# Four norms of a two-block kernel: tokens scaled before they are turned, with new head, tail and decay sums

## The reference, cut to what matters

```python
def rmsnorm(x, g):                      # first block: mixing norm and FFN norm
    y = x * lax.rsqrt(jnp.mean(x * x, axis=-1, keepdims=True) + EPS)
    return y * g
h = rmsnorm_2(x, norm_mix_w) * (1 + sc_m) + sh_m      # second block, from c @ w_ada
z, xbc, dt_raw, q, k, v = jnp.split(h @ w_in, IN_SPLITS_2, axis=-1)
...
a_cs = jnp.cumsum(A, axis=2)                          # decay sums of the SSD scan
seg = a_cs[:, :, :, None] - a_cs[:, :, None]
...
h = rmsnorm_2(x, norm_ffn_w) * (1 + sc_f) + sh_f
x = x + g_f * conv_ffn(h, w_up, ffn_conv_w, w_down)
return rmsnorm_2(x, final_norm_w)
```

## Time and profile before

| | |
|---|---|
| median of 3 runs | 799.52 us (799.29 to 799.68) |
| the profiled execution | 799.78 us |
| its span (first to last instruction) | 797.80 us |
| TensorE busy | 786.4 us, 99% |
| VectorE busy | 599.5 us, 75% |
| ScalarE busy | 489.8 us, 61% |
| granted TensorE clock | 0.998 of full |
| read from HBM | 159.16 MB, 201 GB/s |

### The profile page before, as it was taken

The page is one execution under the profiler, slowest core; times in us unless marked ns, Lnnn a source line. Parts: engine busy times, 40 slices in busy tenths (PEclk is TensorE's granted clock), DMA queues, the critical chain, the costliest instruction groups (busy, mean ns, idle before and its releaser), DMA issues. The chain is left out here.

```text
span 797.8 us, 14220 instructions
## 1 busy us (share of the span) xinstructions
PE 786.4 (99%) x5912; PEld 735.6 (92%) x5912; DVE 599.5 (75%) x803; ACT 489.8 (61%) x746; POOL 17.8 (2%) x38
## 2 busy tenths in 40 slices
PE   8999999999999999999999999999999999999996
PEld 7999979999999889999998888999789999999885
DVE  5576686667876868797878897987968787777463
ACT  6878888567743564444434357767758767665451
POOL 3000001000200000000000000001000000000000
PEclk9999999999999999999999999999999999999999
DMA  8873534456444558898987993634362856555611
GB/s 303 293 245 126 199 124 155 159 180 243 159 159 159 163 208 264 277 303 277 306 289 266 343 373 132 231 107 159 106 211 85 257 163 206 165 170 173 237 53 53
DMA packets 105679, 161.13 MB, mean 202 GB/s; under 512 B 4480, under 2 KB 51856, under 8 KB 105616
## 3 DMA queue, kind: packets, MB, share of 16 engines
q1 hardware_dynamic: 105472, 159.97, 60.4%
q10 hardware_dynamic: 144, 0.26, 0.1%
HBM read 159.16 MB, written 1.06 MB: 201 GB/s over the span
## 5 line engine op out<-in xcount | busy, mean ns | idle before, releaser
L1759 PE MATMUL ps<-p1H,wH 128*128 128x256 f32 x1256 | 358.2, 286 | 1.5 <-issue 0.8
L1111 DVE TENSOR_TENSOR wL<-raw,wH 128x2048 fp32r<-128x2048 f32 (+2 forms) x142 | 284.6, 2009 | 98.4 <-ACT wH L705 94.6
L1759 PE MATMUL ps<-p1H,wL 128*128 128x256 f32 x1256 | 354.8, 283 | 0.0
L1759 PE MATMUL ps<-p1L,wH 128*128 128x256 f32 x1256 | 353.3, 283 | 0.0
L705 ACT ACTIVATE wH<-raw 128x2048 fp32r<-128x2048 f32 (+1 forms) x114 | 212.0, 1864 | 132.2 <-PE ps L1759 77.0
L1759 PEld LDWEIGHTS ps<-p1H,wH 128*128 128x128 f32 x1256 | 240.8, 192 | 5.9 <-issue 3.9
L1759 PEld LDWEIGHTS ps<-p1H,wL 128*128 128x128 f32 x1256 | 240.8, 192 | 0.0
L1759 PEld LDWEIGHTS ps<-p1L,wH 128*128 128x128 f32 x1256 | 240.1, 192 | 0.1
L1762 PE MATMUL ps<-wH,zH 128*128 128x512 f32 x168 | 65.4, 389 | 0.0
L1762 PE MATMUL ps<-wH,zL 128*128 128x512 f32 x168 | 65.4, 389 | 0.0
L1762 PE MATMUL ps<-wL,zH 128*128 128x512 f32 x168 | 65.4, 389 | 0.0
(11 more groups left out here) (296 smaller groups left out, 978.9 us busy)
## 6 DMA issues: line engine op xcount, KB each, us to landing
raw<-in_w_in SPq DMA_DIRECT2D x37, 1024.0 KB, 5.2
raw<-in_w_ada SPq DMA_DIRECT2D x24, 1024.0 KB, 5.2
raw<-in_w_up SPq DMA_DIRECT2D x44, 512.0 KB, 4.9
raw<-in_w_ffn_gate SPq DMA_DIRECT2D x22, 512.0 KB, 4.2
raw<-in_w_ffn_up SPq DMA_DIRECT2D x22, 512.0 KB, 5.6
raw<-in_w_ffn_down SPq DMA_DIRECT2D x10, 1024.0 KB, 5.6
raw<-in_w_down SPq DMA_DIRECT2D x10, 1024.0 KB, 5.2
raw<-in_w_out SPq DMA_DIRECT2D x8, 1024.0 KB, 5.0
```

What stands on the lines that cost most here:

```text
L1111: return v.tensor_tensor(o, a, b, op)
L1759: last = mm(ps[:, t[1], 0:T], wt[:, slot, k, t[2]:t[2] + P], at_[:, k0 + k, :], start=st, stop=en)
```

## The change

- **Norms 0 to 3.** `TMP`, `rb`, `rbs`, `spread` and `late_turn` go. VectorE scales the tokens by `R1` ahead of the turning, in five pieces (`scale_tokens`): token block 0 in two halves, block 1 in 256, 256 and 512 columns. TensorE turns the scaled tokens `US`. ScalarE reads each turned block twice: to `p1H` and, unrounded, to one of three buffers `un_full`, both with the weight (and shift) applied; VectorE subtracts.
- **TensorE's order in a norm.** First token block 0, then block 1 in pairs of k. In norms 1 to 3 all 16 turns stand ahead of the panel; in norm 0 blocks k 4 to 7 are turned inside `q0`. In norm 1 and 3 the second gate sum, in norm 2 the row of the modulation, stand between token block 0 and 1.
- **Head.** Token block 0 comes in two halves on SP, block 1 on ScalarE's queue. SP waits for the first half only. `warm` runs 8 and 2 times instead of 4, 2 and 4.
- **Tail.** In `dd1` the second tile's first parts are closed one panel earlier; VectorE adds them (`all_but_last_part`) ahead of the last panel's first tile. The left half goes to a bank of its own as well. Three of four stores' products are VectorE's; the last one is one operation from `res`, without `HG`.
- **Decay sums.** Four matmuls of 16, 16, 16 and 8 columns.

```diff
+            act.dma_start(res[:, 1], IN["x"][0, P:2 * P, :]).then_inc(on.in_x[2], 16)
...
@@ scalar: norm @@
-                act.wait_ge(on.ut_psum, 4 * n + 1)
-                nc.scalar.activation(TMP[:, 0], un(0), ACT.Copy).then_inc(on.un0_copy, 1)
                 if n == 0:
                     first_hi(0, 0, 1)
+                    act.wait_ge(on.in_par, 16)
...
-                    act.wait_ge(on.tmp_done, 8 * n + k + 1)
-                    if n < 2:
-                        nc.scalar.activation(p1H[:, k], TMP[:, k], ACT.Copy).then_inc(on.uh_done, 1)
-                    else:
-                        nc.scalar.activation(p1H[:, k], TMP[:, k], ACT.Identity,
-                                             bias=shift(n, k)).then_inc(on.uh_done, 1)
-                    if k == 0:
-                        act.wait_ge(on.rb_psum, n + 1)
-                        nc.scalar.activation(rbs, rb, ACT.Copy).then_inc(on.rb_copy, 1)
+                    act.wait_ge(on.ut_psum, 4 * n + k // 2 + 1)
+                    bias = dict(bias=shift(n, k)) if n >= 2 else {}
+                    f = ACT.Identity if n >= 2 else ACT.Copy
+                    nc.scalar.activation(p1H[:, k], un(k), f, scale=gain(n, k), **bias).then_inc(on.uh_done, 1)
+                    if k > 2:
+                        act.wait_ge(on.u_ready, 8 * n + k - 2)
+                    nc.scalar.activation(un_full[k % 3], un(k), f, scale=gain(n, k), **bias).then_inc(on.un_done, 1)
@@ vector: norm @@
+            def scale_tokens(n, j, cs):
+                dve.wait_ge(on.rd_done, 2 * n + j + 1)
...
+                v.tensor_scalar(US[:, j, cs], (Y if n == 2 else res)[:, j, cs], R1[:, j:j + 1], None,
+                                ALU.mult).then_inc(on.us_done, 1)
...
+                scale_tokens(n, 0, half(0))
+                scale_tokens(n, 0, half(1))
                 turn_over(n, 1)
+                scale_tokens(n, 1, slice(0, T))
+                scale_tokens(n, 1, slice(T, W))
+                scale_tokens(n, 1, half(1))
...
                 for k in range(KD):
-                    stt(TMP[:, k], un(k) if k else TMP[:, 0], gain(n, k), rbs if k else rb, ALU.mult,
-                        ALU.mult).then_inc(on.tmp_done, 1)
-                    if k > 1:
-                        low(k - 1)
-                    if n == 0 and 0 < k < 4:
+                    if n == 0 and k < 4:
                         first_lo(0, k, 1, k == 3)
-                    elif n == 0 and k == 5:
-                        first_lo(1, 0, 2, False)
-                    elif n == 0 and k == 6:
-                        first_lo(1, 2, 2, True)
+                    elif n == 0 and k in (5, 6):
+                        first_lo(1, 2 * k - 10, 2, k == 6)
                     elif n == 3 and k in (5, 7) or n == 2 and k == 6:
                         later_lo(n, 0 if k == 5 else 2)
-                low(KD - 1)
+                    low(k)
@@ vector: tail @@
-                        step(tt(gt[:, T:W], o[:, T:W], g[:, T:W], ALU.mult))
-                        step(tt(right, gt[:, T:W], right, ALU.add))
-                        turn_over(n, 0)
...
+            def all_but_last_part(name, n):
+                whole, o = res[:, 1, half(1)], ps[:, GROUPS[name]["tiles"][1][1], :]
+                dve.wait_ge(*USED[PIDX[name, len(GROUPS[name]["parts"]) - 2]])
+                dve.wait_ge(*EV["dd0", 1])
+                step(tt(gt, o, GATE[n - 3][1], ALU.mult))
+                step(tt(whole, gt, whole, ALU.add))
...
-                    scaled(1, 1)
+                    stt(OUT[:, 1, half(1)], res[:, 1, half(1)], R1[:, 1:2], gout[:, half(1)], ALU.mult,
+                        ALU.mult).then_inc(on.out_dve, 1)
@@ tensor: norm @@
+                    if n == 0:
+                        warm(8)
                     if n in GATE_OF:
                         gate_sum(GATE_OF[n], 0)
+                    pe.wait_ge(on.us_done, 5 * n + 1)
+                    turn(range(4), (0,))
                     if n:
+                        pe.wait_ge(on.us_done, 5 * n + 2)
+                        pe.wait_ge(*EV[f"{RES[n]}1", 1])
+                        turn(range(4, 8), (0,))
+                    if n in GATE_OF:
+                        gate_sum(GATE_OF[n], 1)
                     if n == 2:
                         ada_row(1)
+                    for x in range(4 if n else 2):
+                        pe.wait_ge(on.us_done, 5 * n + min(3 + x, 5))
+                        turn((2 * x, 2 * x + 1), (1,)).then_inc(on.ut_psum, 1)
@@ tensor: decay sums @@
-                        for x, terms in enumerate((((M0, 0),), ((M1, 0),), ((SL, 0),), ((SL, 0), (OL, 1)),
-                                                   ((M0, 1),), ((M1, 1),))):
-                            for y, (mat, j) in enumerate(terms):
-                                last = mm(ps[:, 7, 64 + 8 * x:72 + 8 * x], mat[:], ADT[:, j, :], start=y == 0,
-                                          stop=y == len(terms) - 1)
+                        mm(bm[:, 0:5:4], M0[:], ADT[:], start=True, stop=True)
+                        mm(bm[:, 1:6:4], M1[:], ADT[:], start=True, stop=True)
+                        mm(bm[:, 2:4], SL[:], ADT[:, 0:1].broadcast_to([P, 2, 8]), start=True, stop=False)
+                        last = mm(bm[:, 3], OL[:], ADT[:, 1, :], start=False, stop=True)
```

126 lines of the change are left out of this document (46 added, 80 removed).

## The result

| | before | after |
|---|---|---|
| median | 799.65 us (799.29 to 800.17) | 805.20 us (803.18 to 805.78, 5 runs) |
| the profiled execution, its span | 799.78 us, 797.8 us | 803.18 us, 801.5 us |

The ratio is 1.0066 [1.0054, 1.0077]: slower, and outside the range I gave (797.6 to 802.9). The profiled execution is the fastest of the five; the other four took 805.0 to 805.8 us. So there are two things to explain: the 3.7 us between the two spans, and 2 us more that four of five runs have.

A forecast was written before the change was run, and what follows sets the result against it. TensorE, busy 99% of the span, was taken as the bound, with other engines counting only at head, norms and tail. Terms -0.9 - 0.6 + 0.4 + 0.7 + 1.7 + 0.5 = +1.8 gave 801.3 us, range 797.6 to 802.9.

The forecast's parts named there:

- The norm before u0: Fourth norm: ScalarE's chain and VectorE's half weight difference start the fifth block later, +1.7 us, the largest term.
- The norm before xs: Third norm: TensorE idles for the scaled tokens, then turns, row and copy delay the first matmul, +0.7 us.
- The norm before f0: Second norm: first matmul at 291.17 instead of 290.92, block 1 waits 0.45; +0.4 us in all.
- The decay sums: Four matmuls instead of seven, eight instructions remaining at 0.106 us each: -0.6 us.
- The two-pointer reading: ScalarE's PSUM read with weight and shift as pointers: taken at 0.45 us, bounds 0.36 and 0.50.
- Rival 1: The chains stay hidden and only TensorE's own list counts: -2.0 us, 797.5; chance 0.20.
- Rival 2: Costs at their low halves, so no difference: -0.1 us, 799.5 to 800.5; chance 0.30.
- Rival 4: The tail does not shorten because the last store, not VectorE, ends the kernel: 802.2 us; chance 0.04.
- the head: Start of the kernel: ScalarE's chain from the second weight piece delays TensorE's fifth block, +0.5 us.
- rival 3: Input on a second queue delays token block 0 and the weights: head +1.0, 802.0 up to 803 us; chance 0.12.
- The tail's step: End of the kernel: two of VectorE's six last operations go into its idle time, -0.9 us.

The follow-up runs named there:

- after_again: The changed kernel as it is, run six more times for the spread and a second profile: 803.34 us, ratio 1.0043.
- x_on_sp: The changed kernel with the token input read as before, both blocks on SP and nothing on ScalarE's queue: 802.68 us, ratio 1.0031.
- no_pointers: `x_on_sp` with ScalarE's second reading of each turned block a plain copy, without weight and shift: 800.94 us, ratio 1.0012.
- half_the_filling: The changed kernel with 8 unused identity matmuls in TensorE's halt ahead of the turns of the norm before xs: 803.81 us, ratio 1.0045.
- sooner_two_queues: The changed kernel, input still on two queues, with the modulation row and both gate sums moved ahead of the turns: 799.85 us, ratio 0.9999.
- two_queues_alone: The kernel before with only the input read as in the change, block 1 on ScalarE's queue: 801.43 us, ratio 1.0016.

## Why the prediction was wrong

**Right by its own steps.** The norm before u0, the largest term: the fifth block forecast at 611.35 in the time of before, which 2.41 us of shift make 613.76; it started at 613.88, behind the chain that I named, on VectorE's `wL`. The norm before xs, where no weights come late: its turns, forecast from 481.9, start at 481.83 in `after_again` in the time of before, and the stretch is +0.72 for +0.7. The norm before f0 (+0.44 for +0.4) is right in the sum and partly lucky in its parts: the first matmul came 0.44 later and not 0.25, and block 1 then waited 0.15 us or less and not 0.45. The decay sums (-0.67 for -0.6). The two-pointer reading, bounded by rows from 0.36 to 0.50 and taken at 0.45: 0.45. The rule of the Trainium skill that I had set against it ("ScalarE: Activation LUTs", "What ACT_TABLE_LOAD costs") would say 0.49; here the measurement decides for 0.45. Rival 1, the hidden chains, needed the second reading of block 4 to start before 607.5 in the time of before; it started at 609.2. Rival 2, low halves, falls with it. Rival 4 falls: the tail shortened.

**Wrong, the head.** The +0.5 is ScalarE's chain alone, counted from the second weight piece at 9.54 (fifth block at 16.7 where it was 16.2, by the row 16.30). The second queue got nothing in it: I put the delay of block 0 at 0.6 us and let the start of `q0` be swallowed by the chain. The delay was 1.36 us, the chain then hung on the turned tokens (ScalarE's first high part at 10.01, behind TensorE) and not on the weights, and `q0` started 1.46 us later. This is rival 3's mechanism, which I gave 0.12 and kept apart from the forecast instead of in it; its +1.0 was too small as well. `x_on_sp` measures both halves of the term: 0.47 without the second queue, with ScalarE's chain from the weight piece to the full copy of block 4 at 5.02 us for the 5.06 forecast, and 0.97 for the queue. The Trainium skill says in "DMA: Bandwidth & Descriptors", "Issuing engines are not separate DMA queues", that transfers started by several engines run on the same 16 engines and interleave. The trace agrees in that nothing was won: with block 1's 512 KB on ScalarE's queue at the same time, block 0 is whole at 5.75 us, with both on SP one after the other at 4.34.

**Wrong in size, the stretches behind xs and around the tail.** xs was +0.98, of which 0.26 is the late weight difference, a wait that I had put at nothing. Another 0.22 stands behind it that `no_pointers` does not have (22.54 us from the convolution matmul to the decay sums, 22.55 before, 22.77 after), so that is ScalarE's. The tail's step itself was right (-0.95 up to the last issue for -0.9), but I took the stretch behind it and ahead of it as constant: the last panel's tile came 0.18 later and the last transfer took 0.32 more.

**Missing, the 2 us between the groups.** The text said for xs that TensorE is "idle from 479.76" and charged the halt by its length alone. About half of the changed kernel's runs take 2 us more than the others, and in the five runs of the first measurement this moved the median by 2. No rival had such a term. Filling the halt made these runs go away, so the halt probably has a part in them; that what it costs is TensorE's fall to its 1.2 GHz level is inferred from two variants, where the level cost 0.7 and 1.1 us and late weights, which cost 0.5, went before it. The full account of the 2 us stays open. Without them the result would have been 803.2, still 0.3 over my upper end, from the head (0.94 over its term), xs and what is behind it (0.50) and the tail (0.45). The Trainium skill, "TensorE: Matmul & The Clock Gate", "Part 1: The HAM clock gate", says that the number of slow matmuls differs between runs of one kernel. The trace agrees in the head: at the start of `q0` the changed kernel has its matmuls 0.21 us apart until 11.85 us in the first profile and no such stretch in `after_again`. For the groups 2 us apart no run here shows it.

**What the change is worth.** The norms as written cost 3.85 us (0.47 in the head, 0.44, 1.20 with the 0.26 of the late weight difference, and 1.74), the second queue 0.97 in the head, against the 1.1 that decay sums and tail gave back. They need not: with the sums ahead of the turns and the input on SP the same norms give 799.21 us, and 798.86 in the variant with VectorE's order moved. But that includes the tail and the decay sums, and these alone, on the old norms, give 798.53 us. On different chips and with overlapping intervals the two cannot be told apart; the new norms bring nothing that the runs can show.

## What to carry to other kernels

When a change makes the busiest engine wait for a new producer, look for work of that engine's own that can stand in the halt: a row of 1 us and two sums of 0.87 moved ahead of the wait gave back 3.5 us here by the medians (2.9 between the profiles), more than the 2.7 us that they take, since the chain behind starts sooner. Ask of a chain both how long it is and when it starts. And ask of a second queue which transfer is needed first: here it held up exactly that one, by 1.4 us. Before a median of five runs is explained, look at whether the runs lie in groups: here it told only which group had most of the five.

## What the runs showed of the hardware

- Amid dense work TensorE's granted clock fell to 0.50 for about 3 us behind halts of 2.40 and 2.45 us, and stayed at 1.00 behind halts of 1.91 to 2.17 us in other profiles; the lower level cost 0.7 and 1.1 us. Between runs of one kernel the times lie in two groups 2 us apart. What decides between them is open.
- At the start of dense work the same kernel can have the lower level or not. Until 11.9 us it cost nothing in this head, until about 13.6 us it cost 0.9 us.
- Matmuls of 256 columns are 0.21 us apart, as at the 1.2 GHz level, in the head of `half_the_filling`, `sooner_two_queues` and `x_on_sp` while the windows of these profiles give the granted clock there as 1.00. The distance between matmuls is the surer sign.
- One and the same weight transfer of 1 MB (the last of `w_ffn_down`) reached ScalarE 5.3 to 7.3 us after its issue, from profile to profile. Where weights were late, the gate products behind their differences on VectorE were late too: 1.33 us at xs in `two_queues_alone`.
- The last store takes 2.99 to 3.9 us from issue to end. With the change's norms and tail it is 3.22 to 3.31 in the seven profiles whose input came over ScalarE's queue and 3.77 to 3.91 in the five whose input did not. There the issuing instruction alone takes 1.23 to 1.66 us and not 0.4. The reason is open.
